# Another place and another order for the weight rings of a matmul-bound encoder trunk

## What is computed

```python
hn = rms_norm(x, norm_w)
u = einsum("bsd,dn->bsn", hn, w_in) + b_in
q, k, v, o, z_a, gates, glu_a, glu_b, z_b, g_a, g_b = split(u)
# branch A: convolution of width 5 on q and k, a bidirectional mLSTM with 4 heads,
#           sigmoid(o), RMS norm of a head, silu(z_a)
y_a = einsum("bsw,wd->bsd", ya, w_a)
# branch B: glu_a * sigmoid(glu_b), convolution of width 31, layer norm, silu, silu(z_b)
y_b = einsum("bsw,wd->bsd", c, w_b)
merged = sigmoid(g_a) * y_a + sigmoid(g_b) * y_b
x = x + einsum("bsd,de->bse", merged, w_out)
```

## Time and profile before

| | |
|---|---|
| median of 3 runs | 2492.06 us (2492.05 to 2492.18) |
| profiled execution | 2491.69 us, its span 2490.0 us |
| PE busy | 2455.4 us (99%) |
| DVE busy | 1934.5 us (78%) |
| ACT busy | 1317.2 us (53%) |
| DMA queue of the loads | 59.7% of 16 engines' span |
| mean granted clock of TensorE | 0.995 |

### The profile page before, as it was taken

The page is one execution under the profiler, slowest core; times in us unless marked ns, Lnnn a source line. Parts: engine busy times, 40 slices in busy tenths (PEclk is TensorE's granted clock), DMA queues, the critical chain, the costliest instruction groups (busy, mean ns, idle before and its releaser), DMA issues.

```text
span 2490.0 us, 43931 instructions
## 1 busy us (share of the span) xinstructions
PE 2455.4 (99%) x14063; PEld 2141.2 (86%) x14063; DVE 1934.5 (78%) x2872; ACT 1317.2 (53%) x1574; POOL 55.6 (2%) x43
## 2 busy tenths in 40 slices
PE   7999999999999999999989999999999999999998
PEld 6888888888888888888878888888888888888887
DVE  5788989898988786556568888888888887765565
ACT  5545454545465557555354454545454655665543
POOL 2000000000000000000010000000000000000000
PEclk9999999999999999999999999999999999999999
DMA  6666656565656666665546655555565666666654
GB/s 186 178 187 181 183 161 184 165 181 165 181 177 187 191 181 189 189 188 190 171 128 188 194 178 175 172 177 173 170 181 158 190 188 186 178 196 191 185 186 135
DMA packets 447922, 444.95 MB, mean 179 GB/s; under 512 B 17968, under 2 KB 445760, under 8 KB 447808
## 3 DMA queue, kind: packets, MB, share of 16 engines
q1 hardware_dynamic: 447808, 443.74, 59.7%
HBM read 441.59 MB, written 2.10 MB: 178 GB/s over the span
## 4 chain that ended last, share of the span: by engine, by line
PE 95%; issue 2%; DVE 2%; ACT 1%; SPq 0%; DVEq 0%; DMA 0%; ACTq 0%
PE ps L1255 55%; PE ps L1258 27%; PE ps L1274 5%; PE ps L1276 2%; PE px L1414 1%; PE px L1393 1%; PE px L1320 1%; DVE Hs L751 0%; DVE HEAD L1030 0%; PE px L1384 0%; SPq L289 0%; PE px L1334 0%; ACT YC L547 0%; ACT W L389 0%; PE px L1401 0%
## 5 line engine op out<-in xcount | busy, mean ns | idle before, releaser
L1255 PE MATMUL ps<-Hs,W 128*128 128x512 f32 x5120 | 1617.7, 397 | 9.6 <-DVE Hs L751 9.6
L690 DVE TENSOR_TENSOR W<-RAW,W 128x1024 fp32r<-128x1024 f32 x824 | 1018.1, 1243 | 426.0 <-ACT W L389 420.4
L389 ACT CAST W<-RAW 128x1024 fp32r<-128x1024 f32 x832 | 866.5, 1048 | 905.3 <-PE ps L1258 795.1
L1258 PEld LDWEIGHTS ps<-Hs,W 128*128 128x128 f32 x5120 | 963.3, 188 | 227.9
L1258 PE MATMUL ps<-Hs,W 128*128 128x256 f32 x5120 | 1007.2, 278 | 0.0
L1255 PEld LDWEIGHTS ps<-Hs,W 128*128 128x128 f32 x5120 | 781.6, 189 | 15.2 <-DVE Hs L751 11.2
L792 DVE SCALAR_TENSOR_TENSOR ACC<-CP,CWT,ACC 128x256 f32<-128x256 f32 x928 | 388.1, 477 | 0.0
L1255 PE MATMUL ps<-YC,W 128*128 128x512 f32 x1024 | 321.6, 395 | 0.0
L1258 PEld LDWEIGHTS ps<-YC,W 128*128 128x128 f32 x1024 | 192.4, 188 | 45.5
L1258 PE MATMUL ps<-YC,W 128*128 128x256 f32 x1024 | 201.2, 278 | 0.0
L1274 PE MATMUL ps<-W,Hs 128*128 128x512 f32 x512 | 181.4, 399 | 0.0
(11 more groups left out here) (179 smaller groups left out, 978.7 us busy)
## 6 DMA issues: line engine op xcount, KB each, us to landing
RAW<-in_w_in_dram SPq DMA_DIRECT2D x640, 512.0 KB, 3.7
RAW<-in_w_a_dram SPq DMA_DIRECT2D x64, 512.0 KB, 3.3
RAW<-in_w_b_dram SPq DMA_DIRECT2D x64, 512.0 KB, 3.4
RAW<-in_w_out_dram SPq DMA_DIRECT2D x64, 512.0 KB, 4.0
M<-in_x_dram SPq DMA_DIRECT2D x2, 1024.0 KB, 8.4
HEAD<-in_b_in_dram SPq DMA_DIRECT2D x8, 256.0 KB, 3.8
out_dram<-M SPq DMA_DIRECT2D x4, 512.0 KB, 2.7
CP<-in_dw_w_dram SPq DMA_DIRECT2D x3, 128.0 KB, 4.7
```

Of the source, the lines that this page charges most:

```text
L389: nc.scalar.copy(WH[:, c, :, :], RAW[:, c, :, :]).then_inc(hi_made, 1)
L690: v.tensor_tensor(WL[:, c, :, :], RAW[:, c, :, :], WH[:, c, :, :].bitcast(F32), ALU.subtract).then_inc(lo_made, 1)
L1255: mm(ps[:, 2 * q + t, :], WH[:, c, kk, t * P:t * P + P], act_in[:, kt, :], start=(kt == 0), stop=False)
L1258: i = mm(ps[:, 2 * q + t, S:2 * S], WL[:, c, kk, t * P:t * P + P], act_in[:, kt, 0:S], start=False, stop=(kt == KT - 1))
```

## The change

An unused tensor of 112 float32 elements a partition (448 bytes) is allocated between `YC` and `RAW`. It moves `RAW`, `W` and all that follows them up by 448 bytes, which is 64 bytes down modulo 512. In `multiply` the four matmuls of a group are issued as long, short, long, short in place of long, long, short, short. Operands, results and waits of each are the same.

```diff
@@ -47,6 +47,7 @@
 DW_TAPS = 31
 PAD = DW_TAPS // 2
 CW = S + PAD
+SKEW = 112
 EPS = 1e-6
@@ -122,6 +123,7 @@
         X = sb("X", [P, KT, S])
         Hs = sb("Hs", [P, KT, 2 * S], F32R)
         YC = sb("YC", [P, KT, 2 * S], F32R)
+        sb("SKEW", [P, SKEW])
         RAW = sb("RAW", [P, QC, KQ, PC])
         W = sb("W", [P, QC, 2, KQ, PC], F32R)
@@ -1252,11 +1254,10 @@
                         for t in range(2):
-                            mm(ps[:, 2 * q + t, :], WH[:, c, kk, t * P:t * P + P], act_in[:, kt, :],
-                               start=(kt == 0), stop=False)
-                        for t in range(2):
-                            i = mm(ps[:, 2 * q + t, S:2 * S], WL[:, c, kk, t * P:t * P + P],
-                                   act_in[:, kt, 0:S], start=False, stop=(kt == KT - 1))
+                            bank, cols = ps[:, 2 * q + t, :], slice(t * P, t * P + P)
+                            mm(bank, WH[:, c, kk, cols], act_in[:, kt, :], start=(kt == 0), stop=False)
+                            i = mm(bank[:, S:2 * S], WL[:, c, kk, cols], act_in[:, kt, 0:S],
+                                   start=False, stop=(kt == KT - 1))
                     i.then_inc(multiplied, 1)
```

## The result

The changed kernel takes 2518.78 us (median of 4 runs, 2517.45 to 2520.20) against 2492.12 us before: a ratio of 1.0105, 95% interval [1.0091, 1.0119]. It is 1% slower. The forecast was 2420, the range ended at 2505, and the rival (b) had named 2521.

The account below looks back on a forecast made before the run. PE, 99% busy, was taken as the bound through matmul density. 3328 groups x 25 ns = 83 us, less 6 for the heads and 5 for waiting groups, gave 72 us: 2492 - 72 = 2420 us, range 2350 to 2505.

Parts of the forecast that it names:

- (b): Rival: new distance of W is worse, multiply falls into the turned loop's slower form, 29 us lost, 2521 us; chance 0.20.
- The bound: Whole kernel: PE, busy 99% of 2490.0 us, sets the end by how densely matmuls follow each other.
- The covers: Weight ring: 5 us a slot cover DMA, cast and subtraction, priced at nothing; VectorE at 91% could follow a faster PE.
- The order at zero: In multiply, alternating long and short costs nothing by itself; bounds -1 ns and +5 ns a pair.
- The place, 25 ns a group gained: Moving W 64 bytes lower modulo 512 removes half of the 50 ns loss in each group of four matmuls.
- The floor of 646 ns a group: Length of a group of four matmuls without loss, against 696.5 ns in the kernel before.
- Place and order as independent: Order and place of multiply's matmuls priced separately; that they might only work together was said to change no chance.
- (a): Rival: the place is indifferent, PE's two read streams do not disturb each other; 2492 us within 0.2%; chance 0.20.
- (c): Rival: all loss goes, 166 us, and VectorE becomes the bound, giving 20 to 30 us back: 2346 to 2356; chance 0.15.
- Over 698 by (b): Test in the g_B stage: a group of four, 696.5 ns before, would exceed 698 ns if (b) held.
- The gate product should stay at 347: Test: gate product reads Hs and YC, which do not move, so 347 ns a pair was expected in every case.
- The turned loop should change in the same sense: Test: turned loop, with W and Hs at their new distance and roles exchanged, should change like multiply.

Follow-up runs that it names:

- the second run: Only the unused SKEW tensor of 112 elements added to the kernel before, multiply's order left long, long, short, short: 2476.98 us, ratio 0.9939.
- The first run: Only multiply's order changed to long, short, long, short against the kernel before, weight rings left in place: 2506.3 us, ratio 1.0061.
- third run: Kernel before with 64 unused bytes behind each slot of W, giving four distances in one run, order long, long, short, short: 2492.28 us, ratio 0.9997.
- seventh run: Kernel before with SKEW of 16 elements, rings 64 bytes higher, multiply's order left long, long, short, short: 2486.06 us, timed once.

## Why the prediction was wrong, point by point

**The bound: right.** PE's pace sets the end, and the change moved the end through it alone. The covers held: DMA, the casts and the subtractions did not come onto the path, nor did VectorE when the pace rose: in the second run the g_B stage took 176.63 us with DVE 102.98 busy, the calls of the GLU stage kept 345.0 ns a pair as well, and PE's longest wait for one cause was 9.0 us.

**The order at zero, whatever the distance: wrong, and this is the step that failed.** The prediction priced the order alone at nothing and said that order and place might work together but that this "changes no chance". At the new distance the order costs 8.3 ns a pair, 345.0 in the second run against 353.3 in the changed kernel, 42 us in all. That turned a gain of 16 us into a loss of 27. The price of zero was taken from the gate product and the first head's turned loop, 347 ns (rows 8 and 9), while the 353 ns of the second head (rows 10) were kept as an end of the bound. All of these have the alternating order at distance 0. The first run shows that at this distance both paces belong to this order: 346.7 and 353.3 in `multiply` too, 13 us in the middle of its runs. Rows 10 were read as a hint about the place. They were a sample of the new order itself: four of the turned loop's eight pairs of calls in the kernel before have that pace, and it deserved half of the weight.

**The place, 25 ns a group gained: right in sign for the old order, nearly four times too large.** The second run measured 2 x 3.3 = 6.7 ns a group. Half of the loss had been taken between two rows of unlike sign; the row against (the loss grows with the columns) deserved more. The floor of 646 ns a group was reached by nothing: the best is 690.

**Place and order as independent: wrong, the second half of the same step.** At -64 the order of two gains 3.3 ns a pair and the alternating order loses 5.0 against the kernel before. The table may have the crossing at 96 down too, with the other sign, though there the order of two also has the other's 350.0 ns. With the two prices that the first runs found, +13 and -16 us, an account without interaction gives about 2489 us, where 2518.78 were measured. This interaction made the result, and the prediction had no term for it.

**The rivals.** (b) had the size right, 353 ns and 2521 us, and the point at which it decides. Its reason was half right: the distance is worse in the new order only. (a) falls: the Trainium skill, page "SBUF — State Buffer", section "Who interferes with whom", says of the PE's two read ports that they are independent and that it never waits. What moved between the kernel before and the second run is where `W`, and what follows it, stands against `Hs` and `YC`; the pair went from 348.3 to 345.0. The measurement decides: for the operands of these matmuls the place matters. Whether what it changes is a wait at a port, no run shows. (c) falls with the size of the gain.

**The tests that were named.** "Over 698 by (b)" held, 707 ns a group. "The gate product should stay at 347, and if it changes, my account of the place is wrong" was a bad test: it went to 352, because its alternating order has two paces at distance 0 and it happened to enter in the slow one. In the second run, in one execution, it took 346.7 ns in layer 0 and 353.3 in layer 1. "The turned loop should change in the same sense" held, at 353 in all heads.

**What stays open.** Which physical meeting of the two streams makes the paces was not settled; the runs show only that the order of lengths and the distance together decide which paces occur. Nor is it known what makes a kernel enter one pace or the other where it has two, as the alternating order has at distance 0 and at -64 and the order of two at -96. All runs moved `W` and none moved `Hs` and `YC`, so that it is their distance that counts, and not the address of `W`, rests on the turned loop, where the roles are exchanged. The period of 256 bytes rests on one run and one trace. No run took the weight loads away, so their part in the loss is argued, not shown.

## What to carry to other kernels

When PE is at 99% and waits for nobody, its pace itself is a quantity to measure: divide a stage without other work by its count of products and compare stages, heads and layers; two values at the same code mean that an order has more than one pace, and both are its price. Where the stationary and the moving operand stand against each other is worth a percent here, but only together with the order of lengths, so try the grid, not each axis alone. Here that grid gives 2472 us with 64 bytes lower and runs of two everywhere, and 2519 with 64 bytes lower and alternation.

## What the runs showed of the hardware that was not expected

The paces of this product are few and far apart. At the 2.4 GHz level, 345.0, 346.7, 348.3, 350.0 and 353.3 ns are 828, 832, 836, 840 and 848 cycles for 768 columns: steps of 4 cycles, and they come again under other orders and distances (345.8, 348.8, 349.2 and 351.1 lie between them). They did not differ with DVE's load (g_A at 81% and g_B at 58% in rows 6). They came again at 256 bytes of distance, and 32 bytes can be worth 20 cycles: 345.0 at -64 and 353.3 at -96. And a change of distance within a call shows at once: by the third group behind it the intervals are those of the new distance (third run). The turned loop confirms the sign of the distance. With `W` 64 bytes lower its stationary operand stands 64 bytes above its moving one, as in `multiply` with `W` 64 bytes higher, and both have 347 ns in the order of two. The other way round, with `W` 64 bytes higher, its alternating order has 353 ns (seventh run), as `multiply` mostly has with `W` 64 bytes lower.
